# First mixed tile copied out of PSUM, new PSUM banks for pooling and mixing, gate units moved ahead of the second shift, second half of the scale's column made inside the first up unit

## The reference

```python
def modulate(h, shift, scale): return h * (1 + scale) + shift

sh1, sc1, g1, sh2, sc2, g2 = split6(silu(c) @ ada_w + ada_b)        # six rows of 1024
u = modulate(rms_norm(x, mix_pre_g), sh1, sc1)
# 4 groups of 256 channels, windows of 2, 4, 8, 16 tokens
y = concat([(window_mean(u_g, win_g) - u_g) @ pool_w[g] for g in 4 groups]) * pool_scale
x = x + g1 * rms_norm(y, mix_post_g)
f = conv_ffn(modulate(rms_norm(x, ffn_pre_g), sh2, sc2), w_up, conv_w, conv_b, w_down)
x = x + g2 * rms_norm(f, ffn_post_g)
# then a second block: two layers of linear attention with layer norms
```

## Time and profile before

| | us |
|---|---|
| median of 3 runs | 1145.33 (1144.76 to 1145.8) |
| profiled execution, its time | 1145.01 |
| its span in the trace | 1143.2 |
| TensorE busy | 1123.7 (98%) |
| VectorE busy | 548.4 (48%) |
| ScalarE busy | 499.1 (44%) |
| GpSimdE busy | 451.2 (39%) |

### The profile page before, as it was taken

The page is one execution under the profiler, slowest core; times in us unless marked ns, Lnnn a source line. Parts: engine busy times, 40 slices in busy tenths (PEclk is TensorE's granted clock), DMA queues, the critical chain, the costliest instruction groups (busy, mean ns, idle before and its releaser), DMA issues.

```text
span 1143.2 us, 17115 instructions
## 1 busy us (share of the span) xinstructions
PE 1123.7 (98%) x6826; PEld 916.5 (80%) x6826; DVE 548.4 (48%) x882; ACT 499.1 (44%) x692; POOL 451.2 (39%) x346
## 2 busy tenths in 40 slices
PE   8989999999999999999999999999999999999997
PEld 5658888888888888888788878888888888888886
DVE  3672554324452234567986556422200443676825
ACT  3374453544421223875443255744322343534632
POOL 0115544545445471654432211035354444564430
PEclk8999999999999999999999999999999999999999
DMA  9993232332342333433232211122343322223201
GB/s 343 415 384 111 74 110 82 101 110 73 110 128 78 111 111 112 148 110 112 75 108 78 75 37 38 74 74 74 108 125 109 111 79 91 95 75 111 75 1 74
DMA packets 87240, 128.97 MB, mean 113 GB/s; under 512 B 13300, under 2 KB 66306, under 8 KB 86919
## 3 DMA queue, kind: packets, MB, share of 16 engines
q1 hardware_dynamic: 81730, 119.62, 31.0%
q10 hardware_dynamic: 5445, 8.42, 2.1%
HBM read 122.77 MB, written 5.26 MB: 112 GB/s over the span
## 4 chain that ended last, share of the span: by engine, by line
PE 85%; DVE 5%; issue 3%; DMA 2%; ACT 2%; SPq 1%; POOL 1%; DVEq 0%; POOLq 0%
PE ps L295 24%; PE ps L297 24%; PE ps L296 24%; PE ps L1804 3%; DVE conv_v L1339 2%; DMA ada<-in_ada_w 1%; PE ps L2344 1%; DVE diag L1389 1%; PE ps L2345 1%; PE ps L2413 1%; PE ps L2403 1%; POOL wl L443 1%; PE ps L2350 1%; DVE outer L1386 1%; DVE shift_acc L1107 1%
## 5 line engine op out<-in xcount | busy, mean ns | idle before, releaser
L443 POOL TENSOR_TENSOR wl<-raw,wh 128x512 fp32r<-128x512 f32 x312 | 420.5, 1380 | 612.5 <-ACT wh L494 612.5
L295 PE MATMUL ps<-xth,wh 128*128 128x512 f32 (+1 forms) x832 | 324.4, 390 | 1.8 <-DVE xtl L1236 1.4
L297 PE MATMUL ps<-xth,wl 128*128 128x512 f32 (+1 forms) x832 | 317.4, 382 | 0.0
L296 PE MATMUL ps<-xtl,wh 128*128 128x512 f32 (+1 forms) x832 | 317.3, 381 | 0.0
L494 ACT ACTIVATE wh<-raw 128x2048 fp32r<-128x2048 f32 x78 | 149.3, 1914 | 304.9 <-PE ps L297 284.7
L295 PEld LDWEIGHTS ps<-xth,wh 128*128 128x128 f32 x832 | 156.5, 188 | 34.6 <-issue 4.5
L297 PEld LDWEIGHTS ps<-xth,wl 128*128 128x128 f32 x832 | 156.4, 188 | 30.4
L296 PEld LDWEIGHTS ps<-xtl,wh 128*128 128x128 f32 x832 | 156.7, 188 | 28.7 <-issue 0.5
L1244 DVE SCALAR_TENSOR_TENSOR conv_out<-ps,conv_taps,conv_out 128x511 f32<-128x511 f32 x44 | 32.8, 745 | 124.8 <-ACT conv_out L665 124.8
L1339 DVE SCALAR_TENSOR_TENSOR conv_v<-ps,gdn_taps,conv_v 128x511 f32<-128x511 f32 (+2 forms) x96 | 71.8, 748 | 40.2 <-ACT conv_v L733 37.5
L295 PE MATMUL ps<-wh,xth 128*128 128x512 f32 x176 | 69.7, 396 | 0.0
(11 more groups left out here) (368 smaller groups left out, 1628.1 us busy)
## 6 DMA issues: line engine op xcount, KB each, us to landing
ada<-in_ada_w SPq DMA_DIRECT2D x24, 1024.0 KB, 12.8
raw<-in_gdn_w_in SPq DMA_DIRECT2D x24, 1024.0 KB, 5.2
raw<-in_ffn_w_up SPq DMA_DIRECT2D x22, 1024.0 KB, 4.9
raw<-in_gla_w_in SPq DMA_DIRECT2D x12, 1024.0 KB, 5.0
raw<-in_ffn_w_down SPq DMA_DIRECT2D x11, 1024.0 KB, 4.9
raw<-in_gdn_w_out SPq DMA_DIRECT2D x8, 1024.0 KB, 4.9
raw<-in_gla_w_out SPq DMA_DIRECT2D x4, 1024.0 KB, 5.1
xres<-in_x SPq DMA_DIRECT2D x4, 512.0 KB, 5.3
```

Source lines behind the costliest of these rows:

```text
L295: nc.tensor.matmul(o, lh, rh, start=first, stop=False)
L296: nc.tensor.matmul(o, lh, rl, start=False, stop=False)
L297: return nc.tensor.matmul(o, ll, rh, start=False, stop=last)
L443: rest = nc.gpsimd.tensor_tensor(lo[:, part], raw[:, s, part], hi[:, part].bitcast(f32), ALU.subtract)
```

## The change

- The first mixed tile (tt = 0) is copied by ScalarE to SBUF (`first_mixed`) after its root; `add_mixed(0)` reads it there, and `mixed(3)` waits for the copy (`act_ready`, which also takes the place of `c_silu`) in place of `x1_done`.
- The banks of `pool_block`, `mixed_group`, `turn_normed` and the gain units are others, and most waits on banks go with them. TensorE interleaves pooling and mixing and does half of tile 2's groups before the shift's column.
- `mod_row` comes before tile 2's last groups, and g1_row is made by halves; `mixed_shift(1)` comes after the gate's last units; `mixed(3)` comes before the units of the second shift.
- `ada_sum(3)` and the scaling of the fourth tile move from ScalarE to VectorE; the last turned tile is copied by both, half each.
- `gain_sum(1)`, `gain_col(1)` and `gain_turn(1)` move behind the first blocks of `modulated` and into the first up unit, which now loops over k outside and over its two column halves inside.
- Two `keep_busy(2, 5)` and a `keep_busy(2, 2)` come in early, `keep_busy(4, 3)` ahead of the up unit goes. The copy of post1_row comes later in VectorE's order.

The diff, cut to its core:

```diff
...
+    first_mixed = at("first_mixed", PH, [D])
...
+def pool_bank(cb):
+    return 4 + (cb + 1) % 4
+def mixed_tile(tt):
+    return first_mixed[:] if tt == 0 else bank2(mixed_bank(tt))
...
 def mixed_bank(tt):
+    return (2, 4, 6, 2)[tt]
+def turned_bank(tt):
     return (4, 6, 2, 4)[tt]
-def turned_bank(tt):
-    return (6, 2, 4, 6)[tt]
+def gain_bank(half):
+    return (0, 6)[half]
+def gain_cols_bank(half):
+    return (0, 7)[half]
...
-    for tt in range(2):
-        norm_square("y", tt)
-        norm_root("y", tt)
+    norm_square("y", 0)
+    norm_root("y", 0)
+    act.wait_ge(S("pool_in"), 34)
+    nc.scalar.activation(first_mixed[:], bank2(mixed_bank(0)), ACT.Copy).then_inc(S("act_ready"), 1)
+    norm_square("y", 1)
+    norm_root("y", 1)
     high(0, 0, 0)
     norm_square("y", 2)
...
-    act.wait_ge(S("ada_used"), 12)
-    act.wait_ge(S("mod_mm"), 2)
-    act.wait_ge(S("ada_summed"), 2)
-    nc.scalar.activation(ada_part[:, 1, :], ps[:, 1, :], ACT.Copy).then_inc(S("ada_summed"), 1)
...
-    norm_scale(3)
...
-    nc.scalar.activation(pooled[:, :, 2 * P:3 * P], bank2(4).rearrange("p (k n) -> p k n", n=P), ACT.Copy).then_inc(S("pooled_written"), 1)
+    nc.scalar.activation(pooled[:, :, 2 * P:3 * P], bank2(turned_bank(2)).rearrange("p (k n) -> p k n", n=P), ACT.Copy)\
+        .then_inc(S("pooled_written"), 1)
+    act.wait_ge(S("turned"), 4)
+    nc.scalar.activation(pooled[:, 4:KD, 3 * P:T], ps[:, turned_bank(3) + 1, :].rearrange("p (k n) -> p k n", n=P), ACT.Copy)\
+        .then_inc(S("pooled_written"), 1)
...
-    act.wait_ge(S("pooled_written"), TT)
+    act.wait_ge(S("pooled_written"), TT + 1)
...
     V.tensor_copy(pool_scale_row[:], bank2(0)).then_inc(S("vec_done"), 1)
-    v.wait_ge(S("vec_mm"), 2)
-    V.tensor_copy(post1_row[:], bank2(2)).then_inc(S("vec_done"), 1)
...
-        y = bank2(mixed_bank(tt))
+        y = mixed_tile(tt)
+        if tt == 0:
+            v.wait_ge(S("act_ready"), 2)
...
     band_sums()
+    v.wait_ge(S("vec_mm"), 2)
+    V.tensor_copy(post1_row[:], bank2(2)).then_inc(S("vec_done"), 1)
     ada_sum(1)
...
+    v.wait_ge(S("vec_mm"), 3)
+    V.tensor_tensor(g1_row[:, 0:512], ps[:, 0, :], post1_row[:, 0:512], ALU.mult).then_inc(S("vec_done"), 1)
     v.wait_ge(S("mod_mm"), 4)
-    V.tensor_tensor(g1_row[:], bank2(0), post1_row[:], ALU.mult).then_inc(S("mods_done"), 1)
+    V.tensor_tensor(g1_row[:, 512:D], ps[:, 1, :], post1_row[:, 512:D], ALU.mult).then_inc(S("mods_done"), 1)
+    v.wait_ge(S("vec_done"), 3)
     v.wait_ge(S("mods_done"), 3)
     add_mixed(0)
...
     norm("u", 2)
+    ada_sum(3)
     turned_out(0)
     norm("u", 3)
+    v.wait_ge(S("xn_done"), TT + 3)
+    V.tensor_scalar(xn[:, 3, :], xres[:, 3, :], stat[:, 2, 3:4], None, ALU.mult).then_inc(S("xn_done"), 1)
     turned_out(1)
     gain_sum(0)
     mod_col(3, 1, SH2)
+    v.wait_ge(S("turned"), 4)
+    V.tensor_copy(pooled[:, 0:4, 3 * P:T], ps[:, turned_bank(3), :].rearrange("p (k n) -> p k n", n=P)).then_inc(S("pooled_written"), 1)
     gain_col(0)
-    gain_sum(1)
-    turned_out(3)
     v.sem_inc(S("conv_done"), 4)
     v.sem_inc(S("act_done"), 2)
     v.wait_ge(S("mods_done"), 5)
-    v.wait_ge(S("pooled_written"), TT)
+    v.wait_ge(S("pooled_written"), TT + 1)
...
     modulated(0)
-    for k in range(0, KD, 2):
-        if k == 2:
-            gain_col(1)
-            v.wait_ge(S("mods_done"), 6)
-        if k + 2 < KD:
-            modulated(k + 2)
-        for n in (k, k + 1):
-            v.wait_ge(S("pooled_done"), KD + n + 1)
-            V.tensor_tensor(xtl[:, n, :], pooled[:, n, :], xth[:, n, :].bitcast(f32), ALU.subtract).then_inc(S("u_lo"), 1)
+    def modulated_low(n):
+        v.wait_ge(S("pooled_done"), KD + n + 1)
+        V.tensor_tensor(xtl[:, n, :], pooled[:, n, :], xth[:, n, :].bitcast(f32), ALU.subtract).then_inc(S("u_lo"), 1)
+    modulated(2)
+    modulated_low(0)
+    modulated_low(1)
+    gain_sum(1)
+    modulated_low(2)
+    gain_col(1)
+    v.wait_ge(S("mods_done"), 6)
+    modulated(4)
+    modulated_low(3)
+    modulated(6)
+    for n in range(4, KD):
+        modulated_low(n)
...
-            pe.wait_ge(S("mods_done"), 3 + 2 * half)
+            pe.wait_ge(S("mods_done"), 3)
             pe.wait_ge(S("ada_summed"), 2)
+            if half:
+                pe.wait_ge(S("pooled_written"), 2)
...
-        mm.then_inc(S("mod_mm"), 1)
+            mm.then_inc(S("mod_mm") if half else S("vec_mm"), 1)
...
+        if cb == 3:
             pe.wait_ge(S("cols_done"), 5)
...
-            pe.wait_ge(S("pooled_done"), (5, 5, 6, 8)[g])
-        if tt == 2 and g == 0:
-            pe.wait_ge(S("mods_done"), 1)
+            pe.wait_ge(S("pooled_done"), 2 * g + 2)
         if tt == 3 and g == 0:
-            pe.wait_ge(S("x1_done"), 1)
+            pe.wait_ge(S("act_ready"), 2)
...
         mm.then_inc(S("vec_mm"), 1)
+        keep_busy(2, 5)
...
-    pe.wait_ge(S("c_silu"), 1)
-    pe.wait_ge(S("vec_done"), 2)
-    for n in range(3):
-        ada_unit(1, n)
+    pe.wait_ge(S("act_ready"), 1)
+    pe.wait_ge(S("vec_done"), 1)
+    ada_unit(1, 0)
+    ada_unit(1, 1)
     pool_block(0)
     pool_block(1)
+    ada_unit(1, 2)
+    pool_block(2)
+    pool_block(3)
     ada_unit(1, 3)
-    pool_block(2)
+    pe.wait_ge(S("vec_done"), 2)
     mod_col(1, 3, 0)
     mod_col(1, 3, 1)
-    for cb in range(3, KD):
-        pool_block(cb)
-    mixed(0)
-    pe.wait_ge(S("pooled_done"), KD)
+    keep_busy(2, 2)
+    pool_block(4)
+    pool_block(5)
+    pe.wait_ge(S("mods_done"), 1)
+    mixed_group(0, 0)
+    pool_block(6)
+    mixed_group(0, 1)
+    pool_block(7)
+    mixed_group(0, 2)
+    mixed_group(0, 3)
     mixed(1)
+    mixed_group(2, 0)
+    mixed_group(2, 1)
     pe.wait_ge(S("shift_summed"), KD)
     for k in range(KD):
         for c in range(0, P, 32):
             mm = X.matmul(ps[c:c + 32, 1, k:k + 1], shift_acc[:, k * P + c:k * P + c + 32], ones[:, 0:1], start=True, stop=True)
     mm.then_inc(S("mod_mm"), 1)
     ada_unit(2, 0)
-    mixed_group(2, 0)
     pe.wait_ge(S("mods_done"), 2)
...
     mm.then_inc(S("mod_mm"), 1)
-    mixed_group(2, 1)
     ada_unit(2, 1)
     mixed_shift(0)
-    mixed_shift(1)
     ada_unit(2, 2)
     ada_unit(2, 3)
+    mixed_shift(1)
+    mod_row(2, 0)
     mixed_group(2, 2)
-    mod_row(2, 0)
     mixed_group(2, 3)
     mixed_shift(2)
+    mixed(3)
+    mixed_shift(3)
     ada_unit(3, 0)
     ada_unit(3, 1)
-    mixed(3)
-    mixed_shift(3)
+    turn_normed(0)
     ada_unit(3, 2)
     ada_unit(3, 3)
-    turn_normed(0)
     turn_normed(1)
     gain_unit(0, 0)
     mod_col(3, 1, 0)
     mod_col(3, 1, 1)
     gain_unit(0, 1)
     turn_normed(2)
+    turn_normed(3)
     gain_turn(0)
-    turn_normed(3)
     gain_unit(1, 0)
     gain_unit(1, 1)
-    gain_turn(1)
-    pe.wait_ge(S("pooled_written"), 2)
-    keep_busy(4, 3)
...
-        for part in range(2):
+        for k in range(KD):
+            if k == 2:
+                gain_turn(1)
+            pe.wait_ge(S("u_lo"), k + 1)
             for sub in range(2):
-                if part == 0 and sub == 1:
-                    pe.wait_ge(S("mods_done"), 6)
                 c = slice(sub * P, (sub + 1) * P)
-                for k in range(4 * part, 4 * part + 4):
-                    if sub == 0:
-                        pe.wait_ge(S("u_lo"), k + 1)
-                    mm = mm3(ps[:, sub, :], whk[:, k, c], wlk[:, k, c], xth[:, k, :], xtl[:, k, :], k == 0, k == KD - 1)
-                if part == 1:
+                mm = mm3(ps[:, sub, :], whk[:, k, c], wlk[:, k, c], xth[:, k, :], xtl[:, k, :], k == 0, k == KD - 1)
+                if k == KD - 1:
                     mm.then_inc(S("up_half") if sub == 0 else w_used, 1)
...
```

More of the change, by code:

```diff
@@ L582, in _ @@
                     act.wait_ge(S("rows_turned"), 1)
-                    nc.scalar.activation(c_col[:], ps[:, 6, 0:KD], ACT.Silu).then_inc(S("c_silu"), 1)
+                    nc.scalar.activation(c_col[:], ps[:, 6, 0:KD], ACT.Silu).then_inc(S("act_ready"), 1)
                 act.wait_ge(S("x_in"), 16 * (TT - 1))
@@ L594, in _ @@
                 act.wait_ge(S("pool_mm"), 1 + cb + 1)
-                nc.scalar.activation(pooled[:, cb, :], ps[:, 4 + cb % 4, :], ACT.Copy, scale=mod_cols[:, SC1, cb:cb + 1])\
+                nc.scalar.activation(pooled[:, cb, :], ps[:, pool_bank(cb), :], ACT.Copy, scale=mod_cols[:, SC1, cb:cb + 1])\
                     .then_inc(S("pooled_done"), 1)
@@ L648, in _ @@
                 nc.scalar.activation(xth[:, k, :], pooled[:, k, :], ACT.Copy).then_inc(S("pooled_done"), 1)
-                act.wait_ge(S("pooled_written"), TT + k // 2 + 1)
+                act.wait_ge(S("pooled_written"), TT + k // 2 + 2)
                 nc.scalar.activation(xth[:, k + 1, :], pooled[:, k + 1, :], ACT.Copy).then_inc(S("pooled_done"), 1)
@@ L1083, in _ @@
             v.wait_ge(S("rows_turned"), 1)
-            v.wait_ge(S("c_silu"), 1)
+            v.wait_ge(S("act_ready"), 1)
```

(19 more changed lines are left out.)

## The result

The changed kernel took 1148.42 us (median of 8 runs, 1148.05 to 1149.85), the kernel before it 1145.26 (8 runs): ratio 1.0034 [1.0025, 1.0044]. It is slower by 0.34%, above the 0.2% that count as a difference, and above the range of the prediction (1141.2 to 1147.0). The profiled execution took 1149.29 us with a span of 1147.5, 4.3 us more than before; by the sum it should have been 1.7 us less, so 6.0 us of span are to be explained.

The account below looks back on a forecast made before the run. TensorE was taken as the bound, running without a gap from the second up unit's start at 90.08 us. With 4.1 us won at `modulated(0)` less 2.4 given back, 1.7 us gained: 1143.6 us, range 1141.2 to 1147.0.

Parts of the forecast that it names:

- the sum: Whole forecast: second up unit at 88.4 instead of 90.08 us, 4.1 won less 2.4 given back, 1.7 us gained.
- Start, up to the column of the first scale: Vector rows, fillers, first ada units: fillers hold the clock, columns turned from 26.4 us against 26.24, +0.1 us.
- the clock isn't held at the start: Rival: columns, shift chain and gate unit 4 come 2.5 us later, 1145.3 to 1146; chance 0.11, shared with a landing's take-up.
- The mixing, and from there to the norms: Pool blocks to norm inversions: shift column 40.9, gate units end 1.6 us earlier, third root inverted 0.8 us earlier at 55.5.
- S: Start of VectorE's `modulated(0)`, forecast near 71.9 us against 76.04 before, 4.1 us earlier.
- The first up unit: Late second gain turn makes ScalarE wait 2.4 us and TensorE stand some 2.5 us before the second up unit.
- unit 1: The second up unit; TensorE was forecast to start it at S + 16.5 = 88.4 us, against 90.08 before.
- Sum, behind unit 1: Total from the second up unit's start: 1.7 us gained, as moving that start moves the end by as much.
- a rival for the clock at this place: Clock falls ahead of the first up unit: +3.2 us, second up unit at 91.6, 1146.8 us; chance 0.14.

Follow-up runs that it names:

- e6: Changed kernel with the same four start filler matmuls in one block behind both vector rows, not between them: 1144.96 us, ratio 1.0009 to the kernel before.
- e5: Kernel before the change with only the two start filler pairs added, one after each vector row: 1148.0 us, ratio 1.0035 to the kernel before.
- e10: The kernel of e8 with GpSimdE's rest of unit 0 held back until the first tile is added: 1138.84 us, one run.
- e4: Changed kernel with the second gain turn one block earlier in the first up unit, at k = 1: 1146.35 us, ratio 1.0021 to the kernel before.
- e7: Changed kernel with gain_turn(1) ahead of the first up unit and gain_sum(1) moved too: 1146.14 us, ratio 1.0016 to the kernel before.
- e1: Changed kernel without the two filler pairs after the vector rows: 1142.56 us, ratio 0.9992 to the kernel before.
- a1: Changed kernel again, unedited, on the chip of the experiments: 1149.19 us, ratio 1.0046 to the kernel before.
- e8: Changed kernel with the second gain turn ahead of the first up unit and no fillers after the vector rows: 1140.01 us, ratio 0.9962 to the kernel before.
- e2: Changed kernel with ScalarE rounding the second up unit while it waits for the scale's second half: 1149.68 us, ratio 1.006 to the kernel before.
- e3: Changed kernel with the edit of e2 and without the start fillers: 1143.69 us, ratio 0.9999 to the kernel before.
- e9: The kernel of e8 without the filler pair ahead of pool block 4 as well: 1141.23 us, ratio 0.9973 to the kernel before.

## Why the prediction was wrong, by its steps

*Start, up to the column of the first scale: failed, in its size and in its reason.* The sum there was +0.1 us at the columns, and they came 5.2 us late. I costed the fillers by their own passes and by the clock that they would hold. The runs show three terms. First, the two rows stop sharing their time: eight passes in 1.99 us before and in e6, 1.98 for four once a filler stands between (changed kernel, e5), 2.0 us lost. Second, the clock falls in spite of them (0.51 in the changed kernel and 0.55 in e5 from 15 to 21 us, 0.53 in e6 from 15 to 18), and it falls over longer work: 3.78 us for a row of 1.98, and 2.08 for four filler passes of 1.21, 2.7 us together. The kernel before has that fall too (0.50), so this is a loss against the forecast and not all of it against that kernel. Third, a pair of them takes 1.21 and not 1.0: 0.4. Together 5.1, the distance from 17.4 to 22.46. What was wrong in the reading is that I took 1.99 us x8 as 0.25 us a pass without asking why these passes cost half of others of 512 columns in float32; the gate row's four took 1.98 (53.68 in the profile after). The trace tells it inside the rows: from 12.40 to 12.45 us the kernel before has two passes in flight, the changed kernel one. My reason for the clock, "the fillers are full 128x128 products, which held 1.00 up to 14 us", was no evidence: in that same trace the clock fell some 3 us behind those fillers.

This is the rival "the clock isn't held at the start", at a chance of 0.11, and that rival too was priced too low: 2.5 us, for it reckoned with the clock alone. e5 settles that these two fillers are enough for the whole 0.35%.

*The mixing, and from there to the norms: right in direction.* From the shift column to S the forecast had 31.0 us, measured 30.0 (before 36.0). Third root inverted 14.0 us behind the column (forecast 14.6), third to fourth normed tile 2.74 (2.75), from the fourth root to S 3.8 (4.0). From the column on the reordering is worth 6.0 us, 1.8 of them the two groups that now lie ahead of the column; this is why S stands only 0.23 later than before, although the column is 6.25 later. The copy out of PSUM had no cost in the sum; it made the sum 2.18 us instead of 1.22, and the third root's inverse waited for that sum, not for the root. It cost about 0.3 us (e10, one run). I also wrote that two ada units would still be in flight when the issues of units 18 and 19 moved; in one-microsecond windows the DMA share is down to 0.03 to 0.17 between 62 and 65 us. Neither TensorE nor VectorE waits for those units there, so no cost shows.

*The first up unit: right.* ScalarE's wait 2.43 (2.4), unit 1 at S + 16.56 (16.5), ended by GpSimdE. e4 moves the turn by one block and takes 1.36 us off the wait and 1.35 off the start; e7 moves it ahead and both are gone. The chain that I named is the cause.

*Sum, behind unit 1: a term missing.* I let the time behind the gap run as before. The gap of 2.2 us is followed by a stretch at half clock, at a cost of 1.6 us, in the profiled executions of the changed kernel, of e1 (0.71 in 86 to 90) and of e6, and not in that of a1; the gaps of 1.27 (e4) and 0.2 us (e7, e8) are not. So it is a term that comes in some executions, three of the four that were traced with this gap. I had a rival for the clock at this place, but ahead of the unit and not behind it, and that one did not happen: 1.00 from 22 to 90. The Trainium skill, TensorE: Matmul & The Clock Gate, section HAM oscillation, tells of an array that is throttled after waiting, so that each burst starts cold. Its waits are longer than this one of 2.2 us, so it does not give this fall as the page states it; but it names the kind of cost that I had not asked for at the gap that I forecast myself. In the prediction I had read the fall at 15 us as agreeing with that section, and this was wrong. The kernel before, in one window:

```profile
14.00:15.00 1.00, 1.00 (x30) 0.90 (x32) 0.73 (x1) 0.98 (x3) 0.00 (x0) 0.96 1.00 377
```

The clock was already falling there while TensorE was busy for the whole microsecond; its wait of 1.24 us until 16.73 came after.

The sum of the miss: start +5.35 (46.25 for 40.9), reordering -1.0, S to unit 1 +0.06, clock behind the gap +1.6, together 6.0 us, the difference between 1147.5 and the forecast span of 1141.5. Without the error at the start it would have been 1143.6 + 1.6 - 1.0 = 1144.2, inside the range; e1's ratio on this kernel's own time says nearly the same, 0.9992 of 1145.26 = 1144.3.

*What stays open.* Whether any filler holds the clock at 15 us: nothing here shows it. The clock fell there in all seven traces with the start fillers, before 21 us in five of the six without them, and not in e1. With a filler between the rows it stayed down for about 7 to 10 us in five traces and for 3 in e4; with none there, for 3 to 4 us in five, for 7 in the kernel before and not at all in e1. So the fillers may even lengthen the fall, but one trace for each kernel doesn't settle it. Nor is it known why the clock fell behind the gap of 2.2 us in three executions and not in a1. The gaps of 2.87 us in e2 and e3 had a fall too, the waits of 2.08 and 2.09 us in the kernel before and e5 had none. And in e2, e8 and e9 it fell between 28 and 39 us as well, where TensorE had waited 1.2 us at most. What starts the fall was not separated.

## What to carry to other kernels

Before a filler goes between two small matmuls, hold the price of one pass against its like elsewhere in the trace: if it is half, the passes may be sharing the array, and here a full-size product between them ended that. A wait forecast for TensorE can have a second price behind it, the clock, so move what causes it even where the wait alone would be paid for by an earlier gain. And work moved into an idle stretch must be asked whose ports it takes: here a wait of ScalarE was filled, and VectorE became late by as much or more.
